# Writing out the mixer's rounds, with named waits in place of two barriers, in a two-layer hybrid trunk

## What is computed

```python
def layer(x, mod, P, l, rope, ctx_k, ctx_v, s0):
    sh_a, sc_a, g_a, sh_f, sc_f, g_f = jnp.split(mod, N_MOD, axis=-1)   # mod = silu(c) @ w_ada + b_ada
    h = rmsnorm(x, ng[0]) * (1 + sc_a) + sh_a
    q, k, v, cb, cc, ch, ur = jnp.split(h @ P['w_in'][l], SPLIT_IN, axis=-1)
    attn = attention(q, keys, vals)                    # 8 heads, 2 key heads
    conv = cb * short_conv(cc * ch, P['conv_w'][l])    # width 3
    rw, S = rwkv_mixer(ur, s0, P, l)                   # 8 heads of 64, two directions
    o = jnp.concatenate([attn, conv, rw], axis=-1) @ P['w_out'][l]
    x = x + g_a * rmsnorm(o, ng[1])
    h = rmsnorm(x, ng[2]) * (1 + sc_f) + sh_f
    ff = (silu(h @ P['w_gate'][l]) * (h @ P['w_up'][l])) @ P['w_down'][l]
    return x + g_f * rmsnorm(ff, ng[3]), k, v, S

def step(S, inp):                                      # one token of rwkv_scan
    sa = einsum('bhij,bhj->bhi', S, -kk_t)
    S = S * w_t + sa[..., None] * (kk_t * a_t) + v_t[..., None] * k_t
    return S, einsum('bhij,bhj->bhi', S, r_t)
```

## Time and profile before

| | |
|---|---|
| median of 3 runs | 3115.71 us (3115.05 to 3121.76) |
| the profiled execution, own time | 3113.37 us |
| its span, first to last instruction | 3111.3 us |
| TensorE products busy | 2836.9 us, 91% of the span |
| VectorE, ACT, POOL busy | 52%, 36%, 5% |
| mean granted TensorE clock | 0.947 of full |
| layer 0's mixer, layer 1's mixer | about 353 to 692 us, 1888 to 2219 us |

### The profile page before, as it was taken

How to read it: one execution, slowest core, us unless ns; L and a number is a source line. 1 busy time by engine, 2 the same in 40 slices (tenths; PEclk the granted TensorE clock), 3 DMA queues, 4 the chain that set the end, 5 groups by cost and what they waited for, 6 DMA issues and landing times. The chain is left out here.

```text
span 3111.3 us, 45973 instructions
## 1 busy us (share of the span) xinstructions
PE 2836.9 (91%) x17315; PEld 2160.7 (69%) x17315; DVE 1623.0 (52%) x2108; ACT 1114.1 (36%) x1441; POOL 165.6 (5%) x209
## 2 busy tenths in 40 slices
PE   6899888879799999999978997888889999999997
PEld 1578554558677777777856885455668888888885
DVE  0465544444555555555555655555445555555554
ACT  0344322224433333333424442222345444444442
POOL 1000111110000000000001001111000000000000
PEclk9899988889899999999988998888999999999998
DMA  9765665655377777776634555666545666666662
GB/s 365 249 181 156 198 207 185 205 175 191 110 221 238 231 230 243 241 226 220 185 115 126 165 154 185 212 218 212 182 145 161 186 188 187 188 189 189 188 188 89
DMA packets 317256, 600.86 MB, mean 193 GB/s; under 512 B 23184, under 2 KB 29288, under 8 KB 316584
## 3 DMA queue, kind: packets, MB, share of 16 engines
q1 hardware_dynamic: 309488, 592.90, 60.0%
q10 hardware_dynamic: 7608, 5.60, 0.6%
HBM read 595.28 MB, written 3.15 MB: 192 GB/s over the span
## 5 line engine op out<-in xcount | busy, mean ns | idle before, releaser
L834 PE MATMUL bank<-hiW,actH 128*128 128x512 f32 (+1 forms) x2304 | 901.4, 391 | 18.0 <-DVE loW L1339 15.8
L834 PE MATMUL bank<-loW,actH 128*128 128x512 f32 (+1 forms) x2304 | 892.1, 387 | 0.0
L834 PE MATMUL bank<-hiW,actL 128*128 128x512 f32 (+1 forms) x2304 | 891.9, 387 | 0.0
L1339 DVE TENSOR_TENSOR loW<-rawW,hiW 128x1024 fp32r<-128x1024 f32 x348 | 425.7, 1225 | 437.9 <-ACT hiW L408 437.6
L408 ACT ACTIVATE hiW<-rawW 128x1024 fp32r<-128x1024 f32 x348 | 368.1, 1060 | 559.6 <-PE bank L834 557.8
L834 PEld LDWEIGHTS bank<-hiW,actH 128*128 128x128 f32 x2304 | 434.7, 189 | 127.4 <-issue 37.0
L834 PEld LDWEIGHTS bank<-hiW,actL 128*128 128x128 f32 x2304 | 434.2, 188 | 88.6
L834 PEld LDWEIGHTS bank<-loW,actH 128*128 128x128 f32 x2304 | 434.6, 189 | 86.7 <-issue 1.0
L1734 DVE TENSOR_TENSOR loW<-rawW,hiW 128x1024 fp32r<-128x1024 f32 x244 | 299.0, 1225 | 337.9 <-ACT hiW L641 337.6
L641 ACT ACTIVATE hiW<-rawW 128x1024 fp32r<-128x1024 f32 x244 | 258.7, 1060 | 447.9 <-PE bank L834 420.0
L834 PE MATMUL bank<-rawW,csR 128*32 128x512 f32 x1536 | 295.5, 672 | 84.0 <-DMA rawW<-in_w_ada 36.2
(11 more groups left out here) (255 smaller groups left out, 2263.9 us busy)
## 6 DMA issues: line engine op xcount, KB each, us to landing
rawW<-in_w_ada SPq DMA_DIRECT2D x384, 512.0 KB, 6.5
rawW<-in_w_gate SPq DMA_DIRECT2D x176, 512.0 KB, 3.7
rawW<-in_w_up SPq DMA_DIRECT2D x176, 512.0 KB, 3.7
rawW<-in_w_down SPq DMA_DIRECT2D x176, 512.0 KB, 3.6
rawW<-in_w_in SPq DMA_DIRECT2D x144, 512.0 KB, 3.6
rawW<-in_w_out SPq DMA_DIRECT2D x64, 512.0 KB, 3.6
rawW<-in_w_in SPq DMA_DIRECT2D x16, 160.0 KB, 2.3
x<-in_x_prompt SPq DMA_DIRECT2D x1, 1024.0 KB, 7.0
```

The source lines that it names most:

```text
L834: return pe.matmul(out, a, b, start=start, stop=stop, skip_group_check=True)
L1339: TT(loW[:, slot, :, 0:width], rawW[:, slot, :, 0:width], hiW[:, c % LEAD, :, 0:width].bitcast(F32), ALU.subtract).then_inc(lo_ready, 1)
```

## The change

- The `Fori` loops of the four rounds become Python loops on all four engines, so that each round's instructions stand in the program and all counters are constants. ACT's and POOL's inner loops over the levels are written out too.
- The barrier before the mixer goes. VectorE waits instead for `u_l` (ACT's copies in `turn_low`), `u_z` (POOL's zeroing of the edges of `uT`) and `u_a`; POOL waits for TensorE's last transposes (`u_T`) before it zeroes `AE` and `BF`; TensorE waits for `u_v` at the mixer's start, and for `lr_act` only behind its first eight adaLN chunks.
- The barrier behind the mixer goes. In the last round ACT rounds the first two chunks of `w_out` ahead of its Square, and VectorE makes their low parts ahead of the variance step. TensorE begins the projection behind the last adaLN rows, after `ST_v`; its second tile also waits for `rw_vs`, and the eighth chunk of every tile for `rw_lo`.
- The five barriers left are renumbered.

```diff
-BARS = 7
+BARS = 5
@@ ACT
-                               bank[4][0:GATE_RANK, 256:512]..., ACT.Copy)
+                               bank[4][0:GATE_RANK, 256:512]..., ACT.Copy).then_inc(u_l, 1)
-                with act.Fori(0, FT) as f:
+                for f in range(FT):
...
-                    with act.Fori(1, LEVELS // 2) as v:
+                    for v in range(1, LEVELS // 2):
...
+                    if f == FT - 1:
+                        hi(l * Q_LAYER + Q_WOUT, 0, 2)
                     act.wait_ge(rw_yc, it + 1)
                     act.activation(yy[1], yy[0], ACT.Square).then_inc(rw_y2, 1)
...
-                phase_end(act, "act", l, 1)
                 rwkv(l)
-                phase_end(act, "act", l, 2)
-                hi(ql + Q_WOUT, 0, 4)
+                hi(ql + Q_WOUT, 2, 4)
@@ POOL
-                pool.memset(uT[:, :, :, 129:130], 0.0)
-                phase_end(pool, "pool", l, 1)
+                pool.memset(uT[:, :, :, 129:130], 0.0).then_inc(u_z, 1)
+                pool.wait_ge(u_T, l * 7 + 7)
+                settle(pool)
                 pool.memset(AE[:], 0.0)
...
-                with pool.Fori(0, FT) as f:
+                for f in range(FT):
...
-                    with pool.Fori(1, LEVELS) as v:
+                    for v in range(1, LEVELS):
@@ TensorE
+            def gemm(s, banks, width=NW, normed=None, mixed=None):
                 for c in range(CPT):
+                    if mixed is not None and c == CPT - 1:
+                        pe.wait_ge(rw_lo, mixed)
...
-                pe.wait_ge(lr_act, l + 1)
+                pe.wait_ge(u_v, l * 3 + 3)
                 settle(pe)
-                with pe.Fori(0, FT) as f:
+                for f in range(FT):
...
                     ada_chunks(qa, 0, 8, 7)
+                    pe.wait_ge(lr_act, l + 1)
                     pe.wait_ge(rw_stage, it + 1)
+                    settle(pe)
...
-                phase_end(pe, "pe", l, 1)
                 rwkv(l)
-                phase_end(pe, "pe", l, 2)
+                pe.wait_ge(ST_v, (l + 1) * FT)
                 for i in range(4):
                     free(l, WIN_TILES + i)
-                    gemm(sl + (S_WOUT + i * 2), (0, 1) if i % 2 == 0 else (2, 3))
+                    if i == 1:
+                        pe.wait_ge(rw_vs, (l + 1) * FT)
+                    gemm(sl + (S_WOUT + i * 2), (0, 1) if i % 2 == 0 else (2, 3), mixed=(l + 1) * FT + 1)
@@ VectorE
+                dve.wait_ge(u_l, l + 1)
+                dve.wait_ge(u_z, l + 1)
+                dve.wait_ge(u_a, l * 3 + 3)
                 lr = ((12, 64, xwa), (13, GATE_RANK, xg))
...
-                with dve.Fori(0, FT) as f:
+                for f in range(FT):
...
                     dve.tensor_copy(rows3[:, 1], bank[3][:]).then_inc(rr_v, 1)
+                    if f == FT - 1:
+                        lo(l * S_LAYER + S_WOUT, 0, 2)
                     dve.wait_ge(rw_yc, it + 1)
                     dve.wait_ge(rw_var, it + 1)
...
-                phase_end(dve, "dve", l, 1)
                 rwkv(l)
-                phase_end(dve, "dve", l, 2)
-                lo(sl + S_WOUT, 0, 4)
+                lo(sl + S_WOUT, 2, 4)
```

More of the change, by code:

```diff
@@ L256, in hybrid_trunk @@
         at_O, at_oa, at_ov, kv_out = sem("at_O"), sem("at_oa"), sem("at_ov"), sem("kv_out")
+        u_l, u_z = sem("u_l"), sem("u_z")
         u_T, u_a, u_v, mix_hi = sem("u_T"), sem("u_a"), sem("u_v"), sem("mix_hi")
@@ L543, in turn_low @@
                 act.activation(uT[0:GATE_RANK, 13, :, 1:129],
-                               bank[4][0:GATE_RANK, 256:512].rearrange("p (g t) -> p g t", g=2), ACT.Copy)
+                               bank[4][0:GATE_RANK, 256:512].rearrange("p (g t) -> p g t", g=2), ACT.Copy).then_inc(u_l, 1)
             def rwkv(l):
@@ L724, in _ @@
                     evac(q + 2, o[:, 1, (2 * i + 1) * NW:(2 * i + 2) * NW], 3)
+                phase_end(act, "act", l, 1)
+                squares(xs, o)
+                phase_end(act, "act", l, 2)
+                squares(xs, x)
+                norm(l * 2 + 1, tf, 3)
+                ffn(l)
                 phase_end(act, "act", l, 3)
@@ L727, in _ @@
                 phase_end(act, "act", l, 4)
[L728 to L733, removed]
             act.dma_start(O["y_prompt"][0], x[:, 0, :]).then_inc(y_out, 16)
@@ L819, in _ @@
                     settle(pool)
+                phase_end(pool, "pool", l, 1)
+                stats(1, l)
                 phase_end(pool, "pool", l, 2)
-                phase_end(pool, "pool", l, 3)
-                stats(1, l)
-                phase_end(pool, "pool", l, 4)
                 pool.memset(o[:], 0.0)
                 stats(2, l)
-                phase_end(pool, "pool", l, 5)
+                phase_end(pool, "pool", l, 3)
                 stats(3, l)
-                phase_end(pool, "pool", l, 6)
+                phase_end(pool, "pool", l, 4)
         @block.tensor
@@ L834, in mm @@
                 return pe.matmul(out, a, b, start=start, stop=stop, skip_group_check=True)
-            def gemm(s, banks, width=NW, normed=None):
+            def gemm(s, banks, width=NW, normed=None, mixed=None):
                 for c in range(CPT):
+                    if mixed is not None and c == CPT - 1:
+                        pe.wait_ge(rw_lo, mixed)
                     if normed is not None:
@@ L1311, in _ @@
                 turn_low(l)
-                phase_end(pe, "pe", l, 1)
                 rwkv(l)
-                phase_end(pe, "pe", l, 2)
+                pe.wait_ge(ST_v, (l + 1) * FT)
                 for i in range(4):
                     free(l, WIN_TILES + i)
-                    gemm(sl + (S_WOUT + i * 2), (0, 1) if i % 2 == 0 else (2, 3))
-                phase_end(pe, "pe", l, 3)
+                    if i == 1:
+                        pe.wait_ge(rw_vs, (l + 1) * FT)
+                    gemm(sl + (S_WOUT + i * 2), (0, 1) if i % 2 == 0 else (2, 3), mixed=(l + 1) * FT + 1)
+                phase_end(pe, "pe", l, 1)
                 residual(l * 2, 2)
-                phase_end(pe, "pe", l, 4)
+                phase_end(pe, "pe", l, 2)
                 norm(l * 2 + 1, xs)
                 ffn(l)
-                phase_end(pe, "pe", l, 5)
+                phase_end(pe, "pe", l, 3)
                 residual(l * 2 + 1, 5)
-                phase_end(pe, "pe", l, 6)
+                phase_end(pe, "pe", l, 4)
         @block.vector
@@ L1866, in _ @@
                     evac(q + 2, o[:, 0, (2 * i + 1) * NW:(2 * i + 2) * NW], 2)
-                phase_end(dve, "dve", l, 3)
+                phase_end(dve, "dve", l, 1)
                 residual(l * 2, 2, 1)
-                phase_end(dve, "dve", l, 4)
+                phase_end(dve, "dve", l, 2)
                 scaled(l * 2 + 1, xs)
@@ L1874, in _ @@
                 ffn(l)
-                phase_end(dve, "dve", l, 5)
+                phase_end(dve, "dve", l, 3)
                 residual(l * 2 + 1, 5, 3)
                 S.end()
-                phase_end(dve, "dve", l, 6)
+                phase_end(dve, "dve", l, 4)
 INS = ["x_prompt", "x_sample", "cache_k", "cache_v", "state_rwkv", "c", "c_ctx", "w_ada", "b_ada", "norm_g", "w_in",
```

## The result

The changed kernel takes **3038.7 us** (median of four runs, 3030.3 to 3043.8) beside 3116.9 of the kernel before on the same chip: ratio 0.9744, 95% interval 0.9719 to 0.9769. In a later comparison it took 3042.1 us beside 3118.8 (0.9748, 0.9733 to 0.9763). It is 77 to 78 us faster. The forecast was 3058, range 3041 to 3080: right in sign, but 2.3 us outside the range, on the quick side (the median of the later comparison lies inside it, so the miss of the range itself is smaller than what runs differ by).

What follows compares the result with a forecast made beforehand. TensorE was taken as last to end, with removable time at seams into, between and out of rounds; 29.7 + 1.0 + 13.6 + 13.0 = 57.3 us off 3115.7 gave 3058, range 3041 to 3080.

Steps and rivals of the forecast that it cites:

- six seams: Between rounds: without TensorE's 5.5 us branch, VectorE's L1682 to the scans shrinks from 63.9 us in all, gaining 29.7.
- register arithmetic in the tails: Ahead of L1678 in six round tails: constants remove 0.17 us of a 0.21 us wait, 1.0 us in all.
- two entrances: Into each layer's first round: chunks ahead of the lr_act wait, no barrier; 13.6 us in two layers (9.4 to 14.6).
- two last tails with the projection: Out of the last round: w_out's fourth chunk ends 6.5 us earlier per layer, 13.0 us in two (7 to 14).
- clock: In the rounds: half clock shifts with each round's place; no sign, two rounds 8 us, all slow or quick 16.
- "stays" rival: At the seams: TensorE's 4 to 5 us have another cause or return, 30 us lost, 3088 us; chance 0.07.
- misses of straight code: Written-out rounds on ACT and VectorE: one exposed code miss per round each, 16 x 5.5 = 88 us, 3146; chance 0.04.
- transfer rival: Ahead of the masked products: six next-tile adaLN chunks arrive late, gain shrinks by 20 us, 3078 us; chance 0.05.
- I take 5.7: At each seam: VectorE's way from L1682 to the scans after the change, chosen where constants leave 5.3 of 5.97 us.
- four long and four short ones: Rounds counted from POOL's copy at L789: four of eight some 4 us longer, laid to the clock's return in the levels.
- rival with 0.12: All rounds get the late clock, as TensorE idles longer before the masked products: 3074 us; chance 0.12.
- rival on the other side: All rounds get the early clock, with no idle 5 us at the seam: 3042 us; chance 0.10.

Runs made afterwards that it cites:

- e1: The kernel before with only TensorE's loop over the rounds written out, other engines' loops and all barriers kept: 3078.8 us (0.9883).
- e3: The kernel before with all loops of the mixer written out and all barriers kept: 3063.5 us (0.9827).
- e7: The changed kernel with TensorE made to wait for VectorE's last product of the old round before the next adaLN chunks: 3077.3 us.
- e10: The changed kernel with TensorE's added wait before the seam's adaLN chunks, filled with nine products that nothing reads: 3076.7 us.
- e11: The changed kernel unaltered, run a second time in a later comparison: 3042.1 us beside 3118.8 (0.9748).
- e8: The changed kernel with five unread TensorE products per round, three before the masked operands' wait and two before the masked blocks': 3027.3 us (0.971).
- e12: The changed kernel with e8's five unread products plus one ahead of the bonus operand's wait and one ahead of the first level: 3011.1 us (0.9661).

## Why the prediction was right and wrong

By its terms, on the profiled pair (69.6 us measured, 57.3 forecast):

| term | forecast | measured |
|---|---|---|
| six seams | 29.7 (28.1 to 32.1) | 35.3 |
| register arithmetic in the tails | 1.0 | 2.6 (six tails of 0.43) |
| two entrances | 13.6 (9.4 to 14.6) | 14.3 |
| two last tails with the projection | 13.0 (7 to 14) | 12.8 |
| clock (all else in the rounds) | no sign | 6.8 |
| outside the mixer | 0 | -2.3 |

The last row is layer 0's beginning and the stretches between the mixers and after them, read by the same marks; the parts add to 69.5, and the spans differ by 69.6. Of the clock's 6.8, scans to masks is 6.2. The low end of the forecast's sum (44.5) leaves out the tails' 1.0; with it, it is 45.5.

**Right: the branch, the order, the overlap.** TensorE's 5.5 us were the branch; the "stays" rival and the misses of straight code (3146) fall with e1 to e3, and no "issue" of some microseconds appeared at a seam on any engine but the overlapped weight loads. The transfer rival falls too: right ahead of the masked products, in all eight rounds, TensorE's wait ended with VectorE's operand and not with a transfer (us in total, times, longest):

```profile
PE bank L835 <- DVE be L1610: 26.7, 8, 4.3
```

The scans were said to follow ACT's last uT copy by 10 us: 9.8 and 10.2. At the last tail the third chunk was put 12.05 us after the mean's product (2222.25 less 2210.2) and came 11.2 us after it (2157.81 less 2146.60). The mean's product, before and after:

```profile
2210.20 0.70 PE L834 MATMUL bank<-sigaa,con 128*128 128x256 f32 x2
2146.60 0.70 PE L835 MATMUL bank<-sigaa,con 128*128 128x256 f32 x2
```

ACT's splits delayed the normalization by 1.5 us, against 1.8 forecast.

**Wrong: the size of the seam.** The step was "I take 5.7", between 5.3 and VectorE's way with registers, 5.97. With registers the way was 5.8 to 6.2 us (e1), as worked out, but with constants it is 4.76, below the low end. That is 0.94 us in each of six seams, 5.6 us. Of the 0.94, 0.44 is the step from the worked-out 5.26 up to 5.7, for which the prediction gives no reason. The other 0.50 was not priced, since I had taken off only the gaps that the trace shows as idle, 0.35 and three times 0.12: 0.21 for the operation that is itself longer when a register addresses its scalar (L1564, 0.56 against 0.35), 0.09 for the overlap ahead of L1552, 0.18 because the copy and the scans were added end to end where each begins before its neighbour has ended (5.97 against e1's 5.79), and 0.02 in other lengths. The same omission sits in the tail: 0.17 us ahead of L1678 was counted, and 0.43 went, because the handshake over actH also shortened (0.74 to 0.48).

**Wrong: the clock had a sign.** The forecast let it go either way within 8 us. The idle that the change removes at the seam is what put the masked products at half clock in the six rounds behind a seam before (11.5 to 12.0 us from scans to masks), as e7 and e10 show; without it five of those six come at 10.3, in the changed kernel as in e3. Scans to masks is 6.2 us shorter in all on this pair, and 10.0 in e3, where both first rounds come at 10.3 too. The forecast had also misread what splits the rounds: of the 4 us between its four long and four short ones, counted from POOL's copy to the end of L1682, 2.6 lie between that copy and the scans, and the first stretch of the levels took 7.8 to 8.9 us in seven of the eight, long and short. The rival with 0.12 had said the opposite, that TensorE would idle longer ahead of the masks; that idle is there (3.1 us in the round behind the seam shown), and in five of eight rounds it did not cost the clock. The rival on the other side (3042, "no idle 5 us at the seam", 0.10) had the right cause, for the masks; but its 16 us were to come from the levels, whose first stretch got no shorter (63.5 and 66.0 us). That the time came out near its 3042 is luck: the seams, the tails and the masks made it up.

Against the medians the rest of the miss is the base: the profiled 3113.4 lay below its median, as the sum allowed for, and the profiled 3043.8 lay 1.7 to 5 us above the medians of the changed kernel. That spread follows the clock: its slowest run has a mean granted clock of 0.958 and its quickest, 3030.3 us, 0.966.

On the table load, the Trainium skill, "ScalarE: Activation LUTs", What ACT_TABLE_LOAD costs, adds a drain of some 1380 ns to a switch. In the entrance shown the sigmoid begins 0.01 us after the load's 1.28 us, and the entrances came out at 14.3 us, near the 13.6 worked out with the load's own duration, not 5.5 us higher: the trace does not agree with it here.

What stays open is which of TensorE's gaps costs the clock in a given round: five of the changed kernel's eight rounds reach the masks at full clock, and seven of e3's, with the same code between seam and masks. The changed kernel run again (e11) has five too, four of them the same.

## What to carry to other kernels

Price a loop's branch on the engine that has it, by its own rows, and then ask what is late next with every register turned into a constant: compare the same kind of operation with a constant and a register operand in the trace, its duration and its overlap with its neighbours, not only the gap shown as idle. A removed wait on TensorE can be worth more than its length where the work behind it ran at half clock, so read the duration of one repeated product on both sides of the wait. When a round's length jumps between a few values, fill TensorE's waits with products that nothing reads, sized by their measured duration so that they end before the operand comes: it gave 26 to 31 us here, on top of the 77 to 78 of the change.

## What the runs showed of the hardware

With two waits of 1.03 and 1.13 us (or 0.45 and 1.62) ahead of the levels, TensorE fell to half clock in seven of e8's eight rounds; with 0.6 us at most at the same places (e12) in none. A wait of 3.1 to 3.2 us ahead of the masks, in turn, left it at full clock in four rounds of the changed kernel and at half in a fifth. I had not expected gaps so short to decide. A product of 128x128 weights over 512 columns in fp32 shows as two records; nine in a row took 0.89 us each (18 records in 7.97 us, e10), and one alone 1.02 to 1.08 (e12). And ACT's table load ahead of wS, there in every round with the loop (e1, seams), is gone when the round's code is straight (e3): one load of 1.28 us less per round, off the path at a seam.
